# A three-pass fp32 block stack on one core: gated FFN values put features-first by block transposes and transfers within SBUF

## The reference, cut to what matters

```python
def swiglu(h, w_up, w_down):                       # h: 256 x 1024
    gate, up = jnp.split(h @ w_up, 2, axis=-1)     # each 256 x 2816
    return (jax.nn.silu(gate) * up) @ w_down       # w_down: 2816 x 1024
```

## Time and profile before

| what | value |
|---|---|
| median of three runs | 1481.89 us |
| the profiled execution | 1478.86 us |
| its span | 1477.0 us |
| PE busy | 1452.9 us, 98% |
| DVE busy | 828.9 us, 56% |
| ACT busy | 687.7 us, 47% |
| transfers | 262.14 MB, mean 177 GB/s |

### The profile page before, as it was taken

How to read it: one execution, slowest core, us unless ns; L and a number is a source line. 1 busy time by engine, 2 the same in 40 slices (tenths; PEclk the granted TensorE clock), 3 DMA queues, 4 the chain that set the end, 5 groups by cost and what they waited for, 6 DMA issues and landing times.

```text
span 1477.0 us, 18731 instructions
## 1 busy us (share of the span) xinstructions
PE 1452.9 (98%) x7412; PEld 1224.2 (83%) x7412; DVE 828.9 (56%) x927; ACT 687.7 (47%) x899; POOL 43.2 (3%) x96
## 2 busy tenths in 40 slices
PE   8999999999999999999999999999999999899997
PEld 6888889988888888888888788888787989788886
DVE  5655565865454555455666464554865565554454
ACT  6545445454444544435445455444544444544442
POOL 1000000000000000000000000000100100000000
PEclk9999999999999999999999999999999999999999
DMA  9755554445555455554444346455433543255551
GB/s 356 260 193 189 181 177 166 171 154 213 178 196 190 152 203 196 189 184 169 171 143 143 114 173 254 174 197 180 176 115 114 189 168 143 100 199 199 181 191 57
DMA packets 38574, 262.14 MB, mean 177 GB/s; under 512 B 4288, under 2 KB 4544, under 8 KB 7648
## 3 DMA queue, kind: packets, MB, share of 16 engines
q1 hardware_dynamic: 37152, 252.85, 48.4%
q0 software_dynamic: 1344, 8.16, 1.4%
HBM read 259.95 MB, written 1.05 MB: 177 GB/s over the span
## 4 chain that ended last, share of the span: by engine, by line
PE 95%; ACT 1%; DVE 1%; SPq 1%; DMA 1%; issue 0%; POOL 0%; POOLq 0%; DVEq 0%; ACTq 0%
PE prod L1001 15%; PE prod L1003 15%; PE prod L1002 15%; PE acc L1001 9%; PE acc L1003 9%; PE acc L1002 9%; PE prod L995 4%; PE prod L996 4%; PE prod L997 4%; PE acc L1168 2%; PE aux L1031 2%; PE acc L1018 1%; DMA raw<-in_weights_dram 1%; PE acc L1187 1%; PE o_bank L1220 1%; ACT acts_h L1319 0%
## 5 line engine op out<-in xcount | busy, mean ns | idle before, releaser
L1489 DVE TENSOR_TENSOR w_lo<-raw,w_hi 128x2048 fp32r<-128x2048 f32 x235 | 538.2, 2291 | 341.3 <-ACT w_hi L1301 341.1
L1301 ACT CAST w_hi<-raw 128x2048 fp32r<-128x2048 f32 x235 | 448.0, 1907 | 293.6 <-PE acc L1003 177.3
L1001 PE MATMUL prod<-w_hi,acts_h 128*128 128x512 f32 x944 | 375.9, 398 | 2.5 <-DVE w_lo L1497 1.7
L1003 PE MATMUL prod<-w_hi,acts_l 128*128 128x512 f32 x944 | 368.8, 391 | 0.0
L1002 PE MATMUL prod<-w_lo,acts_h 128*128 128x512 f32 x944 | 368.4, 390 | 0.0
L1001 PE MATMUL acc<-w_hi,mix_h 128*128 128x512 f32 x600 | 236.7, 395 | 0.3 <-DVE small L1581 0.3
L1003 PE MATMUL acc<-w_hi,mix_l 128*128 128x512 f32 x600 | 233.8, 390 | 0.0
L1002 PE MATMUL acc<-w_lo,mix_h 128*128 128x512 f32 x600 | 233.5, 389 | 0.0
L1001 PEld LDWEIGHTS prod<-w_hi,acts_h 128*128 128x128 f32 x944 | 177.8, 188 | 42.9 <-issue 7.0
L1003 PEld LDWEIGHTS prod<-w_hi,acts_l 128*128 128x128 f32 x944 | 177.5, 188 | 37.7
L1002 PEld LDWEIGHTS prod<-w_lo,acts_h 128*128 128x128 f32 x944 | 177.9, 188 | 35.1 <-issue 0.5
(11 more groups left out here) (255 smaller groups left out, 1220.9 us busy)
## 6 DMA issues: line engine op xcount, KB each, us to landing
raw<-in_weights_dram SPq DMA_DIRECT2D x235, 1024.0 KB, 4.9
raw<-in_weights_dram SPq DMA_DIRECT2D x12, 256.0 KB, 6.6
work<-in_mem_dram POOLq DMA_DIRECT2D x2, 1024.0 KB, 13.4
grow<-in_gain_rows_dram POOLq DMA_DIRECT2D x4, 512.0 KB, 4.4
tabs<-in_tabs_dram POOLq DMA_DIRECT2D x1, 1696.0 KB, 9.4
work<-in_x_t_dram SPq DMA_DIRECT2D x4, 256.0 KB, 6.3
x_res<-in_x_dram SPq DMA_DIRECT2D x1, 1024.0 KB, 8.7
work<-in_mem_t_dram POOLq DMA_DIRECT2D x1, 1024.0 KB, 14.4
```

The lines of the kernel that those rows point to most:

```text
L1001: pe.matmul(out, still_hi, wh, start=first, stop=False, skip_group_check=True)
L1003: return pe.matmul(out, still_lo, wh, start=False, stop=last, skip_group_check=True)
L1301: act.copy(w_hi[:, c % RING], raw[:, c % RAW]).then_inc(hi_done, 1)
L1489: dve.tensor_tensor(w_lo[:, c % RING], raw[:, c % RAW], w_hi[:, c % RING].bitcast(F32), ALU.subtract).then_inc(lo_done, 1)
```

## The change

A function `by_blocks(m)` chooses pairs by their number m, counted through all five parts (0 to 54): all but the last of each part, and none of the first three.

For a chosen pair the values reach `mix_h` and `mix_l` by another way:

1. DVE writes the gated products with each row cut into four groups of 64 columns, the two token halves side by side in each (`mid_cut`, in part 1 of `four`).
2. DVE transposes all 32x32 blocks of that 128x512 in one instruction into `mid_blocks` (part 2), and raises `blocks_turned`.
3. SP puts the blocks in place: 16 transfers within SBUF, each 32 partitions of 128 columns (512 bytes), from `mid_blocks` to `mid_moved_to` (part 3). In SP's queue they stand behind the load of chunk u + 5, and ahead of that of u + 6, with waits on `blocks_turned` and on the `mid_lo` of the pair before.
4. ACT, in the item of the next pair's second up chunk, after its split and ahead of its Silu, waits for all 16 and copies them to `mix_h` in two instructions of 128x256, read in runs of 32 elements. DVE, in the same item, after its split and ahead of its products, makes `mix_l` in two subtractions and raises `mid_lo`.

The rows of the down weights of such a pair are laid out in another order (`block_rows`), on the host, to match the features' new places. SP's loop over the weight loads becomes a written-out list. The wait of DVE on `aux_done` ahead of its products is now on the latest transposes planned before.

```diff
+def by_blocks(m):
+    return m % PAIRS < PAIRS - 1 and m >= 3
...
-            if k_half == 0 and p:
+            if k_half == 0 and p and not by_blocks(self.m + p - 1):
                 self.add("turn_mid", m=self.m + p - 1, aux=self.aux)
                 self.aux += 1
+        if by_blocks(self.m + p):
+            self.moves[self.m + p] = len(self.moves) + 1
+            self.move_behind[self.c - 1 + 2 + RAW] = self.m + p
...
+    elif how == "block_rows":
+        v = w[2 * P * at:2 * P * (at + 1)].reshape(4, 2, 32, D).transpose(0, 2, 1, 3)
+        out.reshape(4, 32, 2, D)[...] = v
...
+        mid_cut = four[:, 1, :].rearrange("p (b t f) -> p t b f", b=4, t=2)
+        mid_blocks = four[:, 2, :]
+        mid_moved_to = four[:, 3, :]
+        moved = mid_moved_to.rearrange("p (a t n j) -> p n t a j", a=4, t=2, n=2)
+        def in_blocks(ap):
+            return ap.rearrange("p (t a j) -> p t a j", t=2, a=4)
...
@@ block.sync
+            for c in range(RAW, N):
                 sp.wait_ge(lo_done, c - RAW + 1)
                 sp.dma_start(raw[:, c % RAW], weights[c]).then_inc(raw_loaded[c % RAW], 16)
+                if c in plan.move_behind:
+                    m = plan.move_behind[c]
+                    sp.wait_ge(blocks_turned, plan.moves[m])
+                    sp.wait_ge(mid_lo, m)
+                    for a in range(4):
+                        for b in range(4):
+                            sp.dma_start(mid_moved_to[32 * b:32 * b + 32, a * P:(a + 1) * P],
+                                         mid_blocks[32 * a:32 * a + 32, b * P:(b + 1) * P]).then_inc(blocks_moved, 16)
...
@@ block.scalar, in the item of a second up chunk, after flush()
+                        m = it["m"] - 1
+                        if m in plan.moves:
+                            tile = MID_TILE + 2 * (m % 2)
+                            act.wait_ge(blocks_moved, 256 * plan.moves[m])
+                            for n in range(2):
+                                ins = act.copy(in_blocks(mix_h[:, tile + n]), moved[:, n])
+                            ins.then_inc(mid_hi, 1)
                         act.wait_ge(rstd_done, it["stat"])
...
@@ block.vector, in the same item, after flush()
+                        if m - 1 in plan.moves:
+                            tile = MID_TILE + 2 * ((m - 1) % 2)
+                            dve.wait_ge(mid_hi, m)
+                            for n in range(2):
+                                ins = dve.tensor_tensor(in_blocks(mix_l[:, tile + n]), moved[:, n],
+                                                        in_blocks(mix_h[:, tile + n].bitcast(F32)), ALU.subtract)
+                            ins.then_inc(mid_lo, 1)
                         dve.wait_ge(rstd_done, it["stat"])
                         for t in range(2):
                             dve.wait_ge(silu_done, 2 * m + t + 1)
-                            if m >= 2 and t == 0:
+                            if it["turned"] and t == 0:
                                 dve.wait_ge(aux_done, it["turned"])
+                            out, up, gate = mid_tok[m % 2][:, t], up_bank(it, t)[:, S:2 * S], gate_s[:, t]
+                            if m in plan.moves:
+                                out = mid_cut[:, t]
+                                up, gate = [a.rearrange("p (b f) -> p b f", b=4) for a in (up, gate)]
+                            dve.scalar_tensor_tensor(out=out, in0=up, scalar=rstd["x"][:, t:t + 1], in1=gate,
+                                                     op0=ALU.mult, op1=ALU.mult).then_inc(mid_done, 1)
+                        if m in plan.moves:
+                            dve.wait_ge(mid_done, 2 * m + 2)
+                            dve.transpose(mid_blocks, four[:, 1, :]).then_inc(blocks_turned, 1)
```

More of the change, by code:

```diff
@@ L136, in __init__ @@
         self.hn = 0
+        self.moves, self.move_behind = {}, {}
     def add(self, kind, **k):
@@ L244, in ffn_down @@
         m = self.m + p
-        item = self.chunk("down", (*source, "rows", p), tiles=[MID_TILE + 2 * (m % 2), MID_TILE + 2 * (m % 2) + 1],
+        item = self.chunk("down", (*source, "block_rows" if by_blocks(m) else "rows", p), tiles=[MID_TILE + 2 * (m % 2), MID_TILE + 2 * (m % 2) + 1],
                           first=(p == 0), last=(p == PAIRS - 1), mid=m, j=self.acc_j, acc_taken=self.acc_taken,
@@ L805, in build @@
         mid_done = sem("mid_done")
+        blocks_turned = sem("blocks_turned")
+        blocks_moved = sem("blocks_moved")
         mid_hi = sem("mid_hi")
@@ L1891, in number @@
                 it["stat"] = last_stat["x"]
-                if it["k_half"] and it["m"] >= 2:
-                    it["turned"] = mid_aux[it["m"] - 2]
+                if it["k_half"]:
+                    it["turned"] = mid_aux[max(mid_aux)] if it["m"] and mid_aux else None
             else:
```

## The result

The changed kernel takes 1486.65 us (median of five, 1484.86 to 1487.63) against 1481.21 us before (median of five, 1479.08 to 1482.81). The ratio is 1.0043, with a 95% interval of 1.0032 to 1.0053: 5.4 us slower, where 14 us faster was forecast. The profiled execution took 1486.93 us, its span 1485.1 us.

The account below looks back on a forecast made before the run. PE, busy 98% of the span, was taken to bound the kernel. 21.0 us of transposes less 4.6 of first-pair stands and 2.4 of clock falls gave 14.0: median 1481.89 becomes 1467.9 us, range 1459.5 to 1478.

Parts of the forecast that it names:

- PE's 0.45 us a pair: PE time that dropping a pair's four transposes saves in the feed-forward stages; 21.0 us over 47 pairs.
- The normal pair: Moved pairs not first in a stage (43): subtractions end 0.08 us before down's first weight load; no loss taken.
- B: Start of chunk u+3, the next pair's second up chunk, where u is the moved pair's second up chunk.
- SP's weight load behind the transfers: SP's load for chunk u+6, queued after the 16 transfers: lands later, but hidden by 2.6 us.
- A: Start of chunk u+1, the one right after the moved pair's second up chunk u.
- s: Time from one of SP's 16 transfer issues to the next; taken as 0.43 us.
- The first pair of a stage: Four moved pairs without a down chunk between: PE stands 15 s - 5.3, 1.1 us each, 4.6 us in all.
- The clock: Possible clock fall behind the four first-pair stands: half of 1.2 us counted each, 2.4 us in all.
- The rule against mine: Skill's rule that initiating a DMA is usually small; here, moved values would land before the first pair's down asks.
- Rival 3: Transfer issue on SP above 0.62 us: stands at four first pairs eat the 21.0 us, slower than before; chance 0.07.
- Rival 1: Transfers all hidden, at the first pairs too, with a step below 0.355 us or shorter landing; 1460.9 us, chance 0.20.

Follow-up runs that it names:

- e3: Changed kernel, but of each pair's 16 transfers SP issues 8 and GpSimd 8 at the same time; 1460.08 us, ratio 0.9867.
- e7: Changed kernel, but blocks go through an HBM scratch tensor in five SP issues (one write, four reads) instead of 16; 1459.47 us, ratio 0.9868.
- e1: Changed kernel, but the first pair of each feed-forward part goes by TensorE's transposes again (43 moved pairs instead of 47); 1463.13 us, ratio 0.9888.
- e5: Changed kernel, but SP issues 12 of each pair's transfers and GpSimd 4; 1465.67 us, ratio 0.9904.
- micro: Separate program, no variant of the kernel: bursts of 16 transfers in several forms and queues; SP took 0.63 us an issue within SBUF.
- e2: Changed kernel, but only the four first pairs (m = 11, 22, 33, 44) are moved, the other 43 use TensorE's transposes; 1501.35 us, ratio 1.0149.
- e6: Changed kernel, but GpSimd issues all 16 transfers of a pair and SP only weight loads; 1484.87 us, ratio 1.0033.
- e4: Changed kernel, but 8 transfers of 32 x 256 instead of 16 of 32 x 128, values landing in wrong places; 1458.10 us, ratio 0.9855.

## Why the prediction was wrong, point by point

**PE's 0.45 us a pair** was right: the period fell from 16.79 to 16.35, and e3 and e7 give back 19.9 and 19.0 of the 21.0. The latency of a transpose (272 ns in the earlier trace rows) would have promised 51 us. The prediction says that the section of the Trainium skill which it names for the like figure (TensorE: Matmul & The Clock Gate, section Part 4: PE-mode transpose) does not call it a latency. That is too strong: the section puts most of that duration to an access latency. That transposes overlap is what the period of the pair shows, 0.45 us for four.

**The normal pair** was right in each of its steps: block transpose 0.71 (taken 0.69), subtractions 0.75, their end at B + 5.16 (B + 5.15), landing at 1.8. PE lost nothing there in 42 of 43 pairs. I had allowed a step of 0.71 us before these pairs stand, and 0.63 kept below it. The one that stood, near 915, had ACT wait 3.4 us for the transfers; it lies in the fourth part, where GpSimd loads 2 MB of memory rows. The two loads were under way from 904.51 to 913.59, and the transfers of that pair landed up to 6.7 us after their issue. e1 and e5 had a stand there too (1.06 and 0.95 us), e3 and e7 had none. I did not test those loads as its cause by themselves.

**SP's weight load behind the transfers** I had put at A + 1.95 + 16 s + 4.9 and wanted at A + 16.3. With 0.633 for s that is A + 17.0, so the cover of 2.6 us was gone and 0.7 us was lacking. In the normal pair the splits have room for it. At the end of a part they don't, which I had not looked at: 0.8 and 1.0 us at two of them.

**The first pair of a stage** is the step that failed, by the size of one term: "so I take 0.43, near the lower end". The step s was 0.633 us. The stand was forecast as 15 s - 5.3, and with 0.633 that formula gives 4.2. The four starts came 4.37, 3.94, 3.84 and 3.80 us late; the mechanism was right and its input was not. Together they make 16.0 us instead of 4.6. The rows behind 0.43 were all loads from HBM, and a load from HBM is cheaper than an issue within SBUF, by a quarter in a burst (0.46 us in micro) and by half alone (0.33 in the earlier trace rows). I had written that no transfer within SBUF was in the trace, used that for a shorter landing, and did not apply it to the price of the issue.

**The clock** went the dear way because the stands were longer. I had counted half of them, at 1.2 us each; all four came with a fall. Each of the first three cost 1.7 us (at the first 6.08 of drift less 4.37), and the one of the fifth part, which began in the stand, 2.8. The 1.2 was misread: the "x10" of a window in the earlier trace rows counts every matmul that overlaps it. The timeline of before has these two starts there,

```profile
1203.03 0.56 PE L1003 MATMUL prod<-w_hi,mix_l 128*128 128x512 f32 x1
...
1206.67 0.39 PE L1003 MATMUL prod<-w_hi,mix_l 128*128 128x512 f32 x1
```

with 9 steps between them in 3.64 us, where 9 x 0.227 = 2.04: a loss of 1.6. Stands of the size forecast would most likely have had no fall: e5's four, up to 1.65 us, had none.

The sum made again: 21.0 - 16.0 - 7.9 = -2.9, less 3.7 for those three places and 1.6 for the fall near 28 us: 8.2 us slower, where the spans say 8.1. (The medians say 5.4; the profiled execution before lies 2.4 us under its median.)

**The rule against mine**, that the time to initiate a DMA is usually small relative to the DMA itself, does not hold for these transfers: 0.63 us of issue each, ten for a pair, against a landing of 1.8 us. That initiating on several engines saves that time on the sequencer, which the same section of the Trainium skill (DMA: Bandwidth & Descriptors, section Issuing engines are not separate DMA queues) says, is what e3 shows.

**The chances.** Rival 3 is what came, issue over 0.62 us, and I had given it 0.07. Its mark was 0.62 and the measure is 0.63. The bounds that I had drawn for s, 0.38 to 0.87, reached over it; a range that took in the whole of a bound with no row of its own kind, as it should, would have ended beyond 1482. Rival 1, all hidden, is what e3 and e7 are.

## What to carry to other kernels

Before many small transfers replace an instruction of the bounding engine, multiply their count by the time that one issue holds its queue, and set the product against the shortest gap between producer and reader, at the start of a loop and not in its middle. A cost that has no row of its own kind (here: both ends in SBUF) keeps its whole bound in the range. If the count is what is late, share it over two queues, or reach the same layout in fewer and larger transfers; or leave the few places with a short gap on the old path, as e1 does.

## What the runs showed of the hardware

- In a burst, an issue of a transfer within SBUF holds SP's queue 0.63 us, for 8 to 64 KB and 16 to 128 rows alike, and ACT's as long for 32 x 128; from HBM to SBUF it is 0.46 us for 32 x 128; within SBUF on GpSimd 0.50 us.
- Bursts on SP and ACT at the same time run at 0.62 and 0.66 us a step: the two queues do not share what costs the time.
- TensorE's clock stayed at full speed behind idle times of 1.1 to 1.65 us in e5 and fell to half behind all eight of 3.6 to 4.3 us in the changed kernel and e2; of e6's four (2.5, 4.4, 2.5, 6.1 us) the first had no fall. In between it went either way at one and the same place: an idle of 1.80 to 1.83 us ahead of the memory values' matmuls (1201.80 before) comes in all nine traces of the program, with a fall behind it before the change, in the changed kernel and in e4, and none in the other six.
- Small transfers within SBUF land after 1.6 to 1.9 us when no 1 MB load is beside them, and after up to 5.0 us when one is, on GpSimd's queue in e6; on SP's in the changed kernel the first of a burst, beside the load ahead of it, lands after 3.9 us in the median.
